# Splitting the down weights of the second expert layer into high and low halves, in a kernel of two chained transformer blocks

## The reference

```python
_, idx = lax.top_k(scores + e_bias.astype(jnp.float32), TOP_K)     # 8 of 64 experts for each token
...
def expert_block(args):
    tok, e = args                       # 128 slots that share one expert
    xb = h_pad[tok]                     # 128 x 1024
    a = jax.nn.silu(xb @ w_gate[e]) * (xb @ w_up[e])    # 128 x 256
    return a @ w_down[e]                # 128 x 1024
```

## Time and profile before

| what | value |
|---|---|
| median of 3 runs | 3752.11 us (3752.1 to 3758.06) |
| profiled execution: its own time | 3757.8 us |
| profiled execution: span from the first to the last instruction | 3756.0 us |
| busy in that span: TensorE | 3456.6 us, 92% |
| VectorE | 2728.4 us, 73% |
| ScalarE | 1250.4 us, 33% |
| GpSimd | 508.3 us, 14% |
| stretch of the section that is changed | about 3040 to 3691 us |

### The profile page before, as it was taken

One profiled execution on the slowest core, in us unless ns is written; L12 is line 12 of the kernel. 1 busy time (PEld: TensorE's weight loads), 2 busy tenths in 40 slices (PEclk: granted clock), 3 DMA queues, 4 the chain that ended last, 5 costly groups with the idle time before them and its releaser, 6 DMA issues.

```text
span 3756.0 us, 51970 instructions
## 1 busy us (share of the span) xinstructions
PE 3456.6 (92%) x20820; PEld 2835.3 (75%) x20820; DVE 2728.4 (73%) x3147; ACT 1250.4 (33%) x1674; POOL 508.3 (14%) x481
## 2 busy tenths in 40 slices
PE   8998999999996999999789999999679789999995
PEld 8996788999994788997556767767577666776774
DVE  8877577888886587876757777777474677777774
ACT  1013121000014211011324655655331345655652
POOL 0000120101001220100001212212130011211210
PEclk9998889999998889999989999999889999999998
DMA  6545333444544333541026999999632169999993
GB/s 244 183 162 194 115 130 135 180 180 180 186 163 172 116 135 132 186 174 68 23 90 221 371 368 359 361 359 371 261 129 101 76 228 340 339 344 335 340 337 126
DMA packets 118804, 799.30 MB, mean 213 GB/s; under 512 B 33808, under 2 KB 34832, under 8 KB 48400
## 3 DMA queue, kind: packets, MB, share of 16 engines
q1 hardware_dynamic: 78480, 735.14, 52.8%
q0 software_dynamic: 39024, 59.61, 4.7%
q10 hardware_dynamic: 1040, 1.05, 0.1%
HBM read 808.77 MB, written 71.83 MB: 234 GB/s over the span
## 4 chain that ended last, share of the span: by engine, by line
PE 55%; DVE 9%; ACT 3%; issue 1%; DMA 1%; POOL 0%; DVEq 0%; SPq 0%; ACTq 0%; POOLq 0%
PE ps L433 51%; PE ps L447 4%; DMA ring<-yd_dram 1%; DVE ring_r L391 1%; DVE arena L2059 1%; DVE ring_r L390 0%; ACT arena L1879 0%; ACT arena L1689 0%; ACT arena L1824 0%; DVE ring_r L2578 0%; ACT arena L1870 0%; DVE mrow L1858 0%; DVE arena L1860 0%; DVE arena_r L516 0%; DVE ring L2421 0%
## 5 line engine op out<-in xcount | busy, mean ns | idle before, releaser
L433 PE MATMUL ps<-arena_r,ring_r 128*128 128x256 f32 (+1 forms) x9968 | 1301.7, 290 | 62.8 <-DVE ring_r L391 23.2
L433 PEld LDWEIGHTS ps<-arena_r,ring_r 128*128 128x128 f32 x9968 | 1250.2, 191 | 99.6 <-DVE ring_r L391 21.0
L433 PE MATMUL ps<-ring_r,arena_r 128*128 128x512 f32 (+1 forms) x2440 | 664.5, 388 | 6.0 <-DVE arena_r L1931 5.1
L433 PEld LDWEIGHTS ps<-ring_r,arena_r 128*128 128x128 f32 x2440 | 443.1, 189 | 97.6 <-DVE arena_r L1931 5.5
L433 PE MATMUL ps<-ring,arena 128*128 128x512 f32 (+1 forms) x1224 | 490.9, 544 | 1.0 <-DVE arena L2613 1.0
L391 DVE TENSOR_TENSOR ring_r<-ring,ring_r 128x4096 fp32r<-128x4096 f32 (+2 forms) x109 | 474.3, 4352 | 3.7
L2578 DVE TENSOR_TENSOR ring_r<-ring,arena_hi 128x2048 fp32r<-128x2048 f32 x154 | 353.0, 2292 | 98.5 <-ACT arena_hi L2623 90.2
L433 PE MATMUL ps<-arena_hi,arena_r 128*128 128x512 f32 x1232 | 406.2, 397 | 0.0
L433 PEld LDWEIGHTS ps<-ring,arena 128*128 128x128 f32 x1224 | 220.2, 191 | 197.5 <-issue 185.2
L390 DVE CAST ring_r<-ring 128x4096 fp32r<-128x4096 f32 (+2 forms) x109 | 271.5, 2490 | 67.1 <-PE ps L433 55.4
L2623 ACT CAST arena_hi<-ring 128x2048 fp32r<-128x2048 f32 x154 | 293.7, 1907 | 14.2 <-ACT arena_hi L2623 0.8
(11 more groups left out here) (326 smaller groups left out, 3200.4 us busy)
## 6 DMA issues: line engine op xcount, KB each, us to landing
ring<-wexp_dram SPq DMA_DIRECT2D x387, 1024.0 KB, 8.1
ring<-stream_dram SPq DMA_DIRECT2D x143, 2048.0 KB, 7.8
ring<-yd_dram SPq DMA_DIRECT2D x7, 2048.0 KB, 16.0
arena<-yd_dram SPq DMA_DIRECT2D x5, 2048.0 KB, 9.8
xd_dram<-arena POOLq DMA_DIRECT2D x6, 512.0 KB, 5.8
consts_sb<-consts_dram SPq DMA_DIRECT2D x1, 2242.0 KB, 15.8
arena<-xd_dram,small POOLq DMA_INDIRECT x129, 10.1
yd_dram<-arena,small POOLq DMA_INDIRECT x129, 8.0
```

Source lines behind the costliest of these rows:

```text
L433: return pe.e.matmul(ps, lhsT=lhsT, rhs=rhs, start=start, stop=stop, skip_group_check=True)
```

## The change

In the section of layer 1 (`split`), the down weights are split like the others. ScalarE casts them in two pieces of 128 x 1024 (one for each half nn of the output columns) into three new buffers; VectorE subtracts the piece nn = 0, GpSimd the piece nn = 1. The turned hidden rows are split as well (two VectorE instructions in place of one copy). TensorE does 12 fp32r matmuls for a block in place of 4 float32 products. Both halves of the result are copied by ScalarE. On ScalarE and VectorE the casts and low halves of a and b stand ahead of the work on the rows. To make room, a and b have 4 high buffers (5 before) and the rows 2 buffers (3 before), so a gather waits for the rows two blocks earlier and is issued up to three blocks ahead. Layer 0 keeps its program.

```diff
+                self.split = l == 1
+                self.rows_ahead = 2 if self.split else 3
...
-                self.hi_at = [...] + [h[:, :] for h in hi_parts]
+                self.hi_at = [...] + [h[:, :] for h in hi_parts[:2 if self.split else 3]]
+                self.down_at = [hi_parts[2][:, 0:1024], hi_parts[2][:, 1024:2048], hi_parts[3][:, :]]
...
+            def raw_down(self, i, nn, of=rings):
+                return v3(self.raw("d", i, of), 1024)[:, :, 512 * nn:512 * nn + 512]
+            def hi_down(self, i, nn):
+                return v3(self.down_at[(2 * i + nn) % len(self.down_at)], 512)
...  TensorE
+            def down_split(i):
+                ah, al = as_r(ATH.v()), as_r(ATL.v())
+                for nn in range(2):
+                    ps = take(pe, K, "y", i, nn)
+                    for k in range(2):
+                        wh, wl = S.hi_down(i, nn)[:, k, :], S.raw_down(i, nn, rings_r)[:, k, :]
+                        pe.wait_ge(*at("left", K, "h", i))
+                        pe.wait_ge(*at(K, "split down", i, nn))
+                        mm(pe, ps[:, :], ah[:, col(k)], wh, k == 0, False)
+                        mm(pe, ps[:, :], ah[:, col(k)], wl, False, False)
+                        ins = mm(pe, ps[:, :], al[:, col(k)], wh, False, k == 1)
+                    ins.then_inc(*pe.mark("ps", K, "y", i, nn))
...
-                    down(i - 1)
+                    (down_split if S.split else down)(i - 1)
...  VectorE
+            for i in range(n + 1 if S.split else 0):
+                if i:
+                    dve.wait_ge(*at(K, "high down", i - 1, 0))
+                    dve.next.tensor_tensor(S.raw_down(i - 1, 0, rings_r), S.raw_down(i - 1, 0), S.hi_down(i - 1, 0).bitcast(F32),
+                                           ALU.subtract).then_inc(*dve.mark(K, "split down", i - 1, 0))
+                if i + 1 < n:
+                    dve_low_half(dve, S, "a", i + 1)
+                    dve_low_half(dve, S, "b", i + 1)
+                    turn(i + 1)
+                if i < n:
+                    gated(i)
+                    dve.wait_ge(*at("ps", K, "h", i))
+                    if i:
+                        dve.wait_ge(*at(K, "used", "d", i - 1))
+                    dve.next.tensor_copy(ah, bank(K, "h", i)[:, 0:256]).then_inc(*dve.mark())
+                    dve.next.tensor_tensor(al, bank(K, "h", i)[:, 0:256], ah.bitcast(F32), ALU.subtract).then_inc(*dve.mark("left", K, "h", i))
...  ScalarE
+        def act_high_down(act, S, i, nn):
+            act.wait_ge(*S.got("d", i))
+            old = 2 * i + nn - len(S.down_at)
+            if old >= 0:
+                act.wait_ge(*at("ps", S.key, "y", old // 2, old % 2))
+            act.next.copy(S.hi_down(i, nn), S.raw_down(i, nn)).then_inc(*act.mark(S.key, "high down", i, nn))
...
+            def result(i, nn):
+                act.wait_ge(*at("ps", K, "y", i, nn))
+                if i >= 2:
+                    act.wait_ge(*S.put_y(i - 2))
+                act.next.copy(YB[i % 2].v(512 * nn, 512), bank(K, "y", i, nn)[:, :]).then_inc(*act.mark("left", K, "y", i, nn))
...
+            for i in range(n + 1 if S.split else 0):
+                if i + 1 < n:
+                    act_high_half(act, S, "a", i + 1)
+                    act_high_half(act, S, "b", i + 1)
+                    turn(i + 1)
+                if i < n:
+                    act_high_down(act, S, i, 0)
+                    silu(i)
+                    act_high_down(act, S, i, 1)
+                if i:
+                    result(i - 1, 0)
+                    result(i - 1, 1)
...  GpSimd
+            def low_down(i):
+                pool.wait_ge(*at(K, "high down", i, 1))
+                pool.next.tensor_tensor(S.raw_down(i, 1, rings_r), S.raw_down(i, 1), S.hi_down(i, 1).bitcast(F32),
+                                        ALU.subtract).then_inc(*pool.mark(K, "split down", i, 1))
+            ahead = S.rows_ahead + 1
...
             for i in range(n + 1):
-                if i + 1 < n and i + 4 < n:
-                    fetch(i + 4)
+                if i + 1 < n and i + ahead < n:
+                    fetch(i + ahead)
                 if i:
                     put(i - 1)
+                if i < n and S.split:
+                    low_down(i)
```

More of the change, by code:

```diff
@@ L271, in build @@
         hi_parts = []
-        for i, o in enumerate((4096, 6144, 8192 + 4096)):
-            hi_parts.append(nc.alloc_sbuf_tensor_at(f"arena_hi{i}", [128, 2048], F32R, offset=arena_at + 4 * o))
+        for i, o in enumerate((4096, 6144, 8192 + 4096, 8192 + 10240)):
+            hi_parts.append(nc.alloc_sbuf_tensor_at(f"arena_hi{i}", [128, 2048 if i < 3 else 1024], F32R, offset=arena_at + 4 * o))
         out_parts = []
@@ L2234, in build @@
         XH = [sub(6144 + 1024 * i, 1024) for i in range(2)]
-        SUM, AT = sub(15360, 512), sub(15872, 256)
+        SUM, AT, ATH, ATL = [sub(15360 + 256 * i, 256) for i in range(4)]
         OH = [sub(512 * i, 512) for i in range(4)]
@@ L2475, in __init__ @@
                 self.place = {it: j for j, it in enumerate(self.items)}
-                self.hi_at = [rings_r[:, 2048 * (NRAW + i):2048 * (NRAW + i) + 2048] for i in range(10 - NRAW)] + [h[:, :] for h in hi_parts]
+                self.hi_at = [rings_r[:, 2048 * (NRAW + i):2048 * (NRAW + i) + 2048] for i in range(10 - NRAW)] + [h[:, :] for h in hi_parts[:2 if self.split else 3]]
+                self.down_at = [hi_parts[2][:, 0:1024], hi_parts[2][:, 1024:2048], hi_parts[3][:, :]]
             def order(self):
@@ L2510, in all_done @@
                     eng.wait_ge(*self.got(*it))
-                for i in range(max(0, self.n - 3), self.n):
+                for i in range(max(0, self.n - self.rows_ahead), self.n):
                     eng.wait_ge(*self.got_x(i))
@@ L2549, in turn_hidden @@
                 ins.then_inc(*pe.mark("ps", K, "h", i))
+            def down_split(i):
[10 more added lines that the diff above has]
+                    ins.then_inc(*pe.mark("ps", K, "y", i, nn))
+                pe.here(K, "used", "d", i)
             def down(i):
@@ L2592, in turn, with gated @@
                     dve.next.tensor_tensor(lo, bank(K, "x", i, g)[:, :], hi.bitcast(F32), ALU.subtract).then_inc(*dve.mark("left", K, "x", i, g))
+            def gated(i):
+                dve.wait_ge(*at(K, "silu", i))
+                a = SUM.v(0, 256)
+                dve.next.tensor_tensor(a, a, bank(K, "hidden", i)[:, 256:512], ALU.mult).then_inc(*dve.mark("left", K, "hidden", i))
             turn(0)
-            for i in range(n + 1):
+            for i in range(n + 1 if S.split else 0):
[9 more added lines that the diff above has]
+                    gated(i)
+                    ah, al = as_r(ATH.v()), as_r(ATL.v())
+                    dve.wait_ge(*at("ps", K, "h", i))
[3 more added lines that the diff above has]
+                    dve.next.tensor_tensor(al, bank(K, "h", i)[:, 0:256], ah.bitcast(F32), ALU.subtract).then_inc(*dve.mark("left", K, "h", i))
+            for i in range(0 if S.split else n + 1):
                 if i + 1 < n:
@@ L2600, in dve_section @@
                 if i < n:
-                    dve.wait_ge(*at(K, "silu", i))
-                    a = SUM.v(0, 256)
-                    dve.next.tensor_tensor(a, a, bank(K, "hidden", i)[:, 256:512], ALU.mult).then_inc(*dve.mark("left", K, "hidden", i))
+                    gated(i)
                 if i:
@@ L2637, in turn, with silu @@
                     act.next.copy(as_r(XH[i % 2].v(512 * g, 512)), bank(K, "x", i, g)[:, :]).then_inc(*act.mark(K, "x high", i, g))
-            turn(0)
-            for i in range(n + 1):
+            def silu(i):
+                act.wait_ge(*at("ps", K, "hidden", i))
+                if i:
+                    act.wait_ge(*at("ps", K, "h", i - 1))
+                act.next.activation(SUM.v(0, 256), bank(K, "hidden", i)[:, 0:256], ACT.Silu, bias=0.0, scale=1.0).then_inc(*act.mark(K, "silu", i))
+            def result(i, nn):
[3 more added lines that the diff above has]
+                act.next.copy(YB[i % 2].v(512 * nn, 512), bank(K, "y", i, nn)[:, :]).then_inc(*act.mark("left", K, "y", i, nn))
+            turn(0)
+            for i in range(n + 1 if S.split else 0):
[7 more added lines that the diff above has]
+                    act_high_down(act, S, i, 1)
+                if i:
+                    result(i - 1, 0)
+                    result(i - 1, 1)
+            for i in range(0 if S.split else n + 1):
                 if i + 1 < n:
@@ L2661, in fetch @@
             def fetch(i):
[L2662 to L2663 removed]
+                if i >= S.rows_ahead:
+                    pool.wait_ge(*at("ps", K, "x", i - S.rows_ahead, 1))
                 pool.e.indirect_dma_start(
[L2665 removed]
+                    out=XB[i % S.rows_ahead].v(), out_offset=None, in_=xd,
                     in_offset=bass.IndirectOffsetOnAxis(ap=TOKEN_OF[:, S.b0 + i:S.b0 + i + 1], axis=0),
[L2667 removed]
```

(11 more changed lines are left out.)

4 lines of the change are left out of this document (2 added, 2 removed).

## The result

The changed kernel takes 3862.95 us (median of 4 runs) beside 3754.86 for the kernel before: a ratio of 1.0289, 95% interval [1.0276, 1.0301]. It is slower, as forecast; 3840 was said for 3863, and the range of 3780 to 3880 holds it. The most likely case's own range, 3821 to 3860, misses it by 3. The profiled execution took 3860.17, 102 more than the one before.

A forecast was written before the change was run, and what follows sets the result against it. TensorE bounds the kernel before; after the change VectorE's ring of 9.68 plus GpSimd's 1.84 gives rounds of about 11.5. 62 x (11.5 - 10.07) = +89, ends -1: 3840 us from 3752.1, 8-in-10 range 3780 to 3880.

The forecast's parts named there:

- The most likely case: GpSimd's low half holds up VectorE each round: P from 11.2 to 11.8, 3821 to 3860 us, 66%.
- The step that decided: GpSimd's low half of down nn=1, 2.38 us, behind the scatter: VectorE's two-SBUF-input subtractions wait for it whole, costing 1.84 a round.
- Both forms of the wait: GpSimd goes ahead of VectorE's down half, costing 1.84 (P 11.52), or between it and a, costing 1.95 (P 11.63).
- The ring of VectorE: VectorE's instructions of a round, 8.45, plus seven gaps of 0.10 and the turn, 0.53: 9.68 us, setting the undisturbed round.
- the wait for the turn: VectorE idles 0.53 a round while TensorE, where free, turns the gated product.
- ScalarE's late cast of a: ScalarE's longer program ends the cast of a 0.17 late for VectorE, 0.09 a round: 9.77; gone in an 11.5 round.
- The fixed point of 11.52: Round length P where GpSimd's start, 12.70 - P in the next round, and VectorE's delay, 13.36 - P, agree: 11.52 us.
- a short fall: Clock rival: TensorE idles 2.1 a round; a short fall costs nothing, half of each round's work at lower level gives 4008, 3%.
- the 89 forecast for the rounds: Layer 1's section: 62 rounds going from 10.07 to 11.5 us, +89 us.
- the rival that the DMA instructions hold VectorE up: GpSimd's two DMA instructions of 1.02 hold VectorE too; with one of them P = 12.6, 3909 us, 5%.

The follow-up runs named there:

- TensorE kept busy: Changed kernel plus ten more 128x128 transposes of the identity a block, in TensorE's wait ahead of the turned hidden rows: 3851.89 us, ratio 1.0259.
- the cast of a ahead: Both layers split, GpSimd's first piece ahead of the scatter; against that kernel, ScalarE's cast of a moved between silu and the second down cast: 3729.56 us, ratio 0.9939.

## Why the prediction was right

**The step that decided held.** VectorE's two-input subtractions wait for GpSimd's, whole. Removing GpSimd's instruction, moving its work to VectorE and moving it in GpSimd's own program each took back what the theory said (3731, 3808 and 3742 to 3755 were expected; 3743, 3812 and 3752 came). Both forms of the wait that the prediction had, ahead of the down half and between that and a, appear.

**The ring of VectorE, 9.68**, came out as 9.65 where nothing disturbs it; the gaps behind its first two instructions are 0.04, not 0.10, and the wait for the turn is 0.59, not 0.53. With the down halves both on VectorE it was 10.97: 1.23 and one gap of 0.10 more.

**ScalarE's late cast of a** was put at 0.17, shared over two rounds, for 9.77. Without GpSimd it was 0.37 in every other round, 9.85. The mechanism was right; the size forecast was half of what was measured.

**The fixed point of 11.52.** The prediction's equation, P = 9.68 + 13.36 - P, ties each round to the one before: the two together take 23.04. Two rounds of 11.52 solve it, and so do 10.54 and 12.50. The prediction took the first and did not see the others; the mean is the same, so with the clock held full it loses nothing by that. With TensorE kept busy the rounds do swing, between 10.5 and 12.5, and 52 of the 61 pairs of neighbours add up to between 22.98 and 23.09. Two rounds of that run near the middle, of 11.40 and 11.66, VectorE and GpSimd (in this kernel's file every line number is two higher):

```profile
3197.47 3.05 DVE L2629 TENSOR_TENSOR ring_r<-ring,arena_hi 128x1024 fp32r<-128x1024 f32 x1
3208.87 3.30 DVE L2629 TENSOR_TENSOR ring_r<-ring,arena_hi 128x1024 fp32r<-128x1024 f32 x1
```

```profile
3197.00 2.42 POOL L2750 TENSOR_TENSOR ring_r<-ring,arena_hi 128x1024 fp32r<-128x1024 f32 x1
3208.67 2.41 POOL L2750 TENSOR_TENSOR ring_r<-ring,arena_hi 128x1024 fp32r<-128x1024 f32 x1
```

The down half ends 1.10 behind GpSimd in both, as forecast (a pass of 1.08), and takes about the 3.0 that was forecast for it. In the changed kernel it doesn't: it takes 1.23 or 1.98, with a mean of 1.76, and the low half of a takes 4.8 in every other round. The other form of the wait, put at 1.95 with no working, cost 2.04 at 3267.50 (6.73 for the two less 4.69).

**What was mis-sized is the clock.** The prediction let a short fall cost nothing, since TensorE would have 2.1 us to spare in each round. The rounds alternate, so the idle is 3.1 us in one and none in the other (1.6 in the mean of the window's rounds, not 2.1); the clock falls behind the long idle, and the slow stretch lands in the short round, which has no slack, and makes the cast of a late in the next. It makes GpSimd late too: ScalarE's last result, put at 10.72 behind the gated product, comes at 12.33 there (3207.41 to 3219.74) and at 10.7 to 10.8 with TensorE kept busy. So GpSimd's low half begins 4.2 into the long round, just behind the recorded start of a, and costs 2.52. The clock costs 0.22 a round by the busy TensorE run, 14 of the 15 us between the 89 forecast for the rounds and the 104 measured. The other 8 between 3840 and 3863 are no mechanism: the forecast took 5.7 off for a profiled execution above its median, and the changed kernel's lies 2.8 under its own.

**Right as well:** TensorE's twelve matmuls take 2.75 (3201.57 to 3204.32), 0.68 less a block, and none of it shows in the time; the transfers fall under 310 GB/s; the two row buffers and four high buffers cost nothing (from 3100 to 3600 no cast of a or b waits for its buffer, three gathers wait for theirs, 0.8 at most, and TensorE waits for none of them). GpSimd's DMA instructions stretch in the meeting (2.90 in place of 1.02, as at 3224.57). But in the run with both halves on VectorE a gather begins inside the two down halves in every round (at 3161.20, for 1.43), and VectorE's low halves keep 1.23 and 2.29 there, so the rival that the DMA instructions hold VectorE up is out.

## What to carry to other kernels

Idle time of GpSimd is not free time: in these runs an elementwise instruction there with SBUF operands cost a VectorE instruction with two SBUF inputs all of its length that was left (2.52 in the long rounds, 0.73 in the short ones), and nothing where VectorE read PSUM or waited. Before such a split, write out VectorE's ring with the gaps between its instructions and place GpSimd's work in its PSUM stretch; here the order of two calls was worth 110 us. A mean over rounds hides an alternation, and slack has to be looked for in the short round, not in the mean.

## What the runs showed of the hardware

**Which of two goes first can't be read from the recorded starts.** Two places of the changed kernel, VectorE and GpSimd:

```profile
3267.50 6.73 DVE L2602 TENSOR_TENSOR ring_r<-ring,arena_hi 128x2048 fp32r<-128x2048 f32 x2 [0.16 <-ACT arena_hi L2667]
...
3290.72 7.63 DVE L2602 TENSOR_TENSOR ring_r<-ring,arena_hi 128x2048 fp32r<-128x2048 f32 x2 [0.25 <-ACT arena_hi L2667]
```

```profile
3268.26 3.82 POOL L2748 TENSOR_TENSOR ring_r<-ring,arena_hi 128x1024 fp32r<-128x1024 f32 x1
...
3291.38 2.42 POOL L2748 TENSOR_TENSOR ring_r<-ring,arena_hi 128x1024 fp32r<-128x1024 f32 x1
```

At 3267.50 VectorE begins 0.76 ahead of GpSimd, goes first, and GpSimd's instruction is stretched to 3.82. At 3290.72 it begins 0.66 ahead and yet waits for all of GpSimd's 2.42 (7.63 for the two, 2.94 more). In the whole section VectorE is recorded as first in 31 meetings: in 27, by 0.21 to 0.73, it waits all the same; in 4, by 0.74 to 0.87, it goes first. The Trainium skill (page "SBUF — State Buffer", section "SBUF: two separate sides") gives the ports to whichever starts first; by the recorded starts the trace agrees at 3267.50 and not at 3290.72. In both places a scatter stands right ahead of GpSimd's instruction. Why GpSimd goes first from behind is open; no run here tells it.

**A gather or scatter on GpSimd's queue waits for a two-input VectorE instruction without holding one up:** 2.90 at 3224.57, ending 0.9 behind the low half of a. With both halves on VectorE the gather of 1.43 at 3161.20 ends 0.9 behind the first down half in the same way, and the two down halves take 2.55, as they do alone.

**More transfers under way did not move more.** In layer 0, 372 GB/s was kept in rounds of 9.84, with 8.9 us from issue to landing. With the cast of a ahead the transfers moved 358, with 12.3 us to landing and rounds of 10.13. By an estimate from the issues (122 and 118 in 400 us) that is 2.7 transfers under way at a time, and 3.6. Why the rate fell is open.
